# Eighteen experts' weights loaded as whole 4 MB matrices in 32 KB rows, instead of half matrices in a ring of nine pieces

## The reference

```python
h = rmsnorm(x, norm2_g)
# a router picks 2 of 32 experts for each token (4 groups of 8), with gates
h_e = silu(xb @ w_gate[e]) * (xb @ w_up[e])      # w_gate, w_up: 2048 x 512
y_e = h_e @ w_down[e]                            # w_down: 512 x 2048
x = x + sum over a token's experts of gate * y_e
out = rmsnorm(x, final_g)
```

## Time and profile before

| | |
|---|---|
| Median of 3 runs | 1319.04 us (1318.78 to 1321.24) |
| Profiled execution's own time | 1319.11 us |
| Its span, first to last instruction | 1317.4 us |
| TensorE busy | 1236.0 us (94%) |
| VectorE, ScalarE busy | 557.3 us (42%), 286.0 us (22%) |
| Moved by DMA | 471.76 MB, mean 358 GB/s over the span |
| Mean granted TensorE clock | 0.984 |

### The profile page before, as it was taken

The page is one execution under the profiler, slowest core; times in us unless marked ns, Lnnn a source line. Parts: engine busy times, 40 slices in busy tenths (PEclk is TensorE's granted clock), DMA queues, the critical chain, the costliest instruction groups (busy, mean ns, idle before and its releaser), DMA issues.

```text
span 1317.4 us, 15705 instructions
## 1 busy us (share of the span) xinstructions
PE 1236.0 (94%) x5942; PEld 647.5 (49%) x5942; DVE 557.3 (42%) x984; ACT 286.0 (22%) x401; POOL 6.0 (0%) x27
## 2 busy tenths in 40 slices
PE   8999999999999999999898899989988999998996
PEld 7888888888874333333333333333333333333332
DVE  6576988774565323232322223223222232232234
ACT  6443454474441011101001000010000000101003
POOL 1000000000000000000000000000000000000000
PEclk9999999999999999999999999999999999999998
DMA  8655454457489999999999999999999999999996
GB/s 306 218 190 178 144 192 162 158 180 300 159 337 344 432 430 430 430 431 432 432 430 430 433 431 432 431 430 432 430 433 431 430 431 432 432 432 430 428 428 251
DMA packets 65985, 471.76 MB, mean 358 GB/s; under 512 B 6135, under 2 KB 6647, under 8 KB 39452
## 3 DMA queue, kind: packets, MB, share of 16 engines
q1 hardware_dynamic: 65948, 471.24, 87.1%
HBM read 469.13 MB, written 2.10 MB: 358 GB/s over the span
## 4 chain that ended last, share of the span: by engine, by line
PE 61%; DMA 33%; DVE 2%; issue 2%; ACT 1%; DVEq 0%; SPq 0%; ACTq 0%
DMA ring<-in_w_up 22%; PE bank L1873 20%; DMA zone_u<-in_w_up 10%; PE bank L1627 10%; PE bank L1635 8%; PE bank L1909 7%; PE bank L1922 5%; PE bank L1636 4%; PE bank L1843 1%; PE bank L1874 1%; DVE zone_u L1056 1%; PE bank L1638 1%; DMA x_tok<-in_x 1%; PE bank L2066 1%; ACT gatesT L867 1%
## 5 line engine op out<-in xcount | busy, mean ns | idle before, releaser
L1873 PE MATMUL bank<-ring,win 128*64 128x512 f32 x816 | 377.3, 617 | 41.5 <-DMA ring<-in_w_up 29.0
L1874 PE MATMUL bank<-ring,win 128*64 128x512 f32 x832 | 378.6, 608 | 0.0
L1873 PEld LDWEIGHTS bank<-ring,win 128*64 128x64 f32 x816 | 111.9, 141 | 284.3 <-issue 265.6
L1635 PE MATMUL bank<-h_both,w_hi 128*128 128x512 f32 x540 | 192.7, 399 | 1.2 <-DVE h_both L978 1.0
L1428 DVE SCALAR_TENSOR_TENSOR x_tok<-bank,gate_of,x_tok 128x512 f32<-128x512 f32 x248 | 169.1, 744 | 30.2 <-PE bank L1922 29.2
L1909 PE MATMUL bank<-ring,hiddenT 128*64 128x512 f32 x672 | 150.8, 594 | 11.3 <-ACT gatesT L867 11.3
L409 DVE TENSOR_TENSOR w_lo<-stage,w_hi 128x2048 fp32r<-128x2048 f32 x58 | 132.5, 2291 | 64.1 <-ACT w_hi L403 64.0
L1636 PE MATMUL bank<-h_both,w_lo 128*128 128x256 f32 x540 | 151.4, 280 | 0.0
L403 ACT ACTIVATE w_hi<-stage 128x2048 fp32r<-128x2048 f32 x58 | 111.3, 1921 | 122.1 <-PE bank L1636 78.5
L859 ACT ACTIVATE rows_now<-bank,root_row 64x512 f32<-64x512 f32 x31 | 21.1, 681 | 533.5 <-PE bank L1874 533.5
L1922 PE MATMUL bank<-y_rows,gatesT 64*128 64x512 f32 x496 | 123.5, 615 | 0.0
(11 more groups left out here) (274 smaller groups left out, 1052.8 us busy)
## 6 DMA issues: line engine op xcount, KB each, us to landing
ring<-in_w_up SPq DMA_DIRECT2D x49, 2048.0 KB, 31.6
ring<-in_w_gate SPq DMA_DIRECT2D x47, 2048.0 KB, 34.9
ring<-in_w_down SPq DMA_DIRECT2D x41, 2048.0 KB, 31.6
stage<-in_w_in SPq DMA_DIRECT2D x43, 1024.0 KB, 5.1
zone_u<-in_w_down SPq DMA_DIRECT2D x19, 2048.0 KB, 31.7
zone_u<-in_w_up SPq DMA_DIRECT2D x9, 2048.0 KB, 33.6
zone_u<-in_w_gate SPq DMA_DIRECT2D x9, 2048.0 KB, 35.0
stage<-in_w_out SPq DMA_DIRECT2D x16, 1024.0 KB, 4.9
```

The lines of the kernel that those rows point to most:

```text
L1635: M.matmul(dst[:, :], hi[:, at], both, start=(c == 0), stop=False)
L1873: M.matmul(dst[0:W_ROWS, :], rows_of[:, c, 0:W_ROWS], gate[:, at], start=(c == 0), stop=(c == C - 1))
L1874: ins = M.matmul(dst[UPPER, :], rows_of[:, c, 0:W_ROWS], up[:, at], start=(c == 0), stop=(c == C - 1))
```

## The change

Experts 0 to 11 are loaded as before (`WIDE = 12`). For experts 12 to 29:

- Each matrix is one transfer of 4 MB, 128 partitions by 32 KB, into a pair of neighbouring buffers. `ring[0]` to `ring[6]` become parts of one tensor `ring_early`, so that pairs are contiguous. There are four pairs: gate of even experts in buffers 0 and 1, gate of odd experts in 7 and 8, up in 5 and 6, down in 2 and 3. Buffer 4 is unused.
- SP's order is gate, up, down of each expert. Gate waits for `down` of the expert two before; up waits for all four quarters of the expert before; down waits for `down` of the expert before.
- TensorE works in another order (`wide_expert`): it first scatters half 0 of the former expert, then waits for the gate matrix and the whole up matrix, does quarters 0 and 1, `turn_gates`, quarters 2 and 3, scatters half 1, `turn_hidden`, `down`.

Experts 30 and 31 get buffers of their own choice (`LAST_SLOTS`) and waits written out by hand; their transfers keep their sizes, their order, and TensorE's order of work, and expert 30's down pieces have semaphores of their own (`former_down`). The final norm's factors, the scratch of the final squares and the buffers of the crowded branch move to other slots.

```diff
-        ring = [sb(f"ring{k}", [P, PIECE]) for k in range(EARLY)]
+        ring_early = sb("ring_early", [P, EARLY * PIECE])
+        ring = [ring_early[:, k * PIECE:(k + 1) * PIECE] for k in range(EARLY)]
...
+LAST_SLOTS = ((0, 1, 4, 7, 8, 5), (6, 2, 3, 0, 1, 4))
+GATE_PAIRS, UP_PAIR, DOWN_PAIR = (0, 7), 5, 2
+WIDE = 12
+ROUNDS = WIDE // ROUND
+WIDE_ROUNDS = (E - 2 - WIDE) // 2
...
+        def pair(k):
+            whole, first = (ring_early, k) if k < EARLY else (zone_u, k - EARLY)
+            return whole[:, first * PIECE:(first + 2) * PIECE]
...
+            with sp.Fori(0, WIDE_ROUNDS) as i:
+                for r in range(2):
+                    e = i * 2 + (WIDE + r)
+                    gate, up, down = (a[n][0][bass.ds(e, 1)].rearrange("e (p x) n -> p (e x n)", p=P)
+                                      for n in ("w_gate", "w_up", "w_down"))
+                    sp.wait_ge(down_used, J * e - J)
+                    sp.dma_start(pair(GATE_PAIRS[r]), gate).then_inc(gate_loaded[r], 16)
+                    sp.wait_ge(in_used, QUARTERS * e)
+                    sp.dma_start(pair(UP_PAIR), up).then_inc(up_loaded, 16)
+                    sp.wait_ge(down_used, J * e)
+                    sp.dma_start(pair(DOWN_PAIR), down).then_inc(down_loaded, 16)
 
             def load_by_halves(e, src):
 
                 for first in (gate_first, gate_last):
-                    for k in (first, first + 1):
-                        wait_used(e + (k - RING) // PIECES, (k - RING) % PIECES)
+                    if e == E - 2:
+                        sp.wait_ge(in_used, QUARTERS * (E - 3 if first == gate_first else E - 2))
+                    else:
+                        sp.wait_ge(down_used, J * (E - 2))
+                        if first == gate_last:
+                            sp.wait_ge(in_used, QUARTERS * (E - 2) + 2)
...
             src = expert_pieces(E - 2)
             load_by_halves(E - 2, src)
-            for k in (down_first, down_last):
-                load_next(E - 2, k, slot_of(E - 2, k), src)
+            for h in range(2):
+                k = down_first + h
+                sp.dma_start(ring[slot_of(E - 2, k)], src[k]).then_inc(former_down[h], 16)
             src = expert_pieces(E - 1)
             load_by_halves(E - 1, src)
-            wait_used(E - 2, 2)
+            sp.wait_ge(in_used, QUARTERS * (E - 2) + QUARTERS)
...
+            def wide_expert(t, gate, of_gate):
+
+                up, weights = pair(UP_PAIR), pair(DOWN_PAIR)
+                banks_free(t - 1, 0)
+                scatter(t - 1, 0, BACK_BANK)
+                pe.wait_ge(win_ready, t)
+                of_gate()
+                pe.wait_ge(up_loaded, 16 * t - 16 * (WIDE - 1))
+                gate_up(t, 0, gate, up, win, whole=True)
+                gate_up(t, 1, gate, up, win, whole=True)
+                turn_gates(t)
+                gate_up(t, 2, gate, up, win, whole=True)
+                gate_up(t, 3, gate, up, win, whole=True)
+                banks_free(t - 1, 1)
+                scatter(t - 1, 1, BACK_BANK)
+                turn_hidden(t)
+
+                def arrived(j):
+                    if j == 0:
+                        pe.wait_ge(down_loaded, 16 * t - 16 * (WIDE - 1))
+
+                down(t, weights[:, 0:PIECE], weights[:, PIECE:], arrived)
+
+            with pe.Fori(0, WIDE_ROUNDS) as i:
+                for r in range(2):
+                    wide_expert(i * 2 + (WIDE + r), pair(GATE_PAIRS[r]), lambda: pe.wait_ge(gate_loaded[r], 16 * i + 16))
```

More of the change, by code:

```diff
@@ L53 @@
 HALVED = (8, 9, 10, 11, 12, 13, 14)
-CROWD_SLOTS = (0, 1, 5, 6, 7, 8)
-FINAL_SLOT = 2
+CROWD_SLOTS = (0, 1, 2, 4, 5, 7)
+FINAL_SLOT = 8
+LAST_SLOTS = ((0, 1, 4, 7, 8, 5), (6, 2, 3, 0, 1, 4))
+GATE_PAIRS, UP_PAIR, DOWN_PAIR = (0, 7), 5, 2
 ROUND = 3
@@ L64 @@
 RETURNS = 2 * BLOCKS
-ROUNDS = (E - 1) // ROUND
+WIDE = 12
+ROUNDS = WIDE // ROUND
+WIDE_ROUNDS = (E - 2 - WIDE) // 2
 assert MOE_BLOCK0 % 3 == 0 and PARTS == 3 and C % STAGES == 0
@@ L304, in hybrid_moe_program @@
         piece_loaded = [sem(f"piece_loaded{k}") for k in range(RING)]
+        gate_loaded = [sem(f"gate_loaded{r}") for r in range(2)]
+        up_loaded = sem("up_loaded")
+        down_loaded = sem("down_loaded")
+        former_down = [sem(f"former_down{h}") for h in range(2)]
         crowd_loaded = [sem(f"crowd_loaded{k}") for k in range(PIECES)]
@@ L377, in piece_at @@
             n = PIECES * e + k
-            assert n != LENT_PIECE
+            assert n != LENT_PIECE and e < WIDE
             if n < FIRST_LOADS:
@@ L385, in slot_of @@
         def slot_of(e, k):
-            return piece_at(e, k)[0]
+            return LAST_SLOTS[e - (E - 2)][k] if e >= E - 2 else piece_at(e, k)[0]
         def load(sp, b, chunks, first=0):
@@ L456, in load_piece @@
             def load_piece(k, src):
-                sp.dma_start(ring[k][:, :], src).then_inc(piece_loaded[k], 16)
+                sp.dma_start(ring[k], src).then_inc(piece_loaded[k], 16)
             gate_first, up_first, gate_last, up_last, down_first, down_last = range(PIECES)
@@ L538, in _ @@
                         load_next(e, k, slot_of(ROUND + r, k), src)
-            assert ROUNDS * ROUND == E - 2
+            assert ROUNDS * ROUND == WIDE and WIDE + 2 * WIDE_ROUNDS == E - 2
+            assert [n for n in (slot_of(WIDE - 1, k) for k in range(3))] == [DOWN_PAIR, UP_PAIR, UP_PAIR + 1]
+            with sp.Fori(0, WIDE_ROUNDS) as i:
[9 more added lines that the diff above has]
+                    sp.dma_start(pair(DOWN_PAIR), down).then_inc(down_loaded, 16)
             def load_by_halves(e, src):
                 for first in (gate_first, gate_last):
-                    for k in (first, first + 1):
-                        wait_used(e + (k - RING) // PIECES, (k - RING) % PIECES)
+                    if e == E - 2:
[4 more added lines that the diff above has]
+                            sp.wait_ge(in_used, QUARTERS * (E - 2) + 2)
                     for h in range(2):
@@ L573, in load_crowd @@
                 for k, src in enumerate(expert_pieces(e)):
-                    sp.dma_start(ring[CROWD_SLOTS[k]][:, :], src).then_inc(crowd_loaded[k], 16)
+                    sp.dma_start(ring[CROWD_SLOTS[k]], src).then_inc(crowd_loaded[k], 16)
             with sp.If(flag > 0):
@@ L900, in final_square @@
                 n = 2 * half + tile
-                nc.scalar.activation(ring[4][:, (BLOCKS * h + n) * NB:(BLOCKS * h + n + 1) * NB], x_tok[:, h, n * NB:(n + 1) * NB], ACT.Square,
+                nc.scalar.activation(ring[6][:, (BLOCKS * h + n) * NB:(BLOCKS * h + n + 1) * NB], x_tok[:, h, n * NB:(n + 1) * NB], ACT.Square,
                                      accum_out=sq_final[:, h, n:n + 1]).then_inc(done, 1)
@@ L1866, in sort, with gate_up @@
                         sort_part(c, t, z)
-            def gate_up(t, q, gate, up, rows_of, into=IN_BANK, part=range(C // QUARTERS)):
-                half, dst = (q % 2) * PART, bank[into]
+            def gate_up(t, q, gate, up, rows_of, into=IN_BANK, part=range(C // QUARTERS), whole=False):
+                half, dst = (q if whole else q % 2) * PART, bank[into]
                 for i in part:
@@ L2047, in _ @@
             turn_hidden(e)
-            down(e, piece(e, 4), piece(e, 5), arrived_down(e))
+            down(e, piece(e, 4), piece(e, 5), lambda j: pe.wait_ge(former_down[j // 2], 16))
             def last_turn(z):
```

## The result

The changed kernel takes 1329.49 us (median of 6 runs, 1324.44 to 1333.19), the one before 1319.22 beside it: ratio 1.0072, 95% interval 1.0061 to 1.0083. It is slower, as forecast, but by 10.3 us and not by 3.6, and outside the range. Its runs lie 9 us apart, those of before 2.5. The profiled execution took 1329.80 us, its span is 1328.1 us, 10.7 more than before.

The account below looks back on a forecast made before the run. DMA bytes were taken to bound the kernel up to expert 29's start, TensorE's work after it. Terms −2.1 + 9.7 − 1.9 − 1.8 − 0.3 = +3.6 us gave 1322.7 us, range 1320.0 to 1327.5.

Parts of the forecast that it names:

- What bounds the kernel, and where the end is decided: DMA bytes bound the experts' stretch; the end depends on expert 29's start and TensorE's work behind it.
- Term 1: Transfers before expert 29: 32 KB rows take 9.685 us per matrix for 9.725, over 53 transfers −2.1 us.
- Term 2: Quarter 0 of wide experts waits for the whole up matrix: +9.7 us, paid at expert 29.
- Term 3: Expert 29, start to scatter of half 1: scatter of half 0 leaves, −1.9 us; quarters at full clock, −1.8 us.
- the clock at expert 29: TensorE idles 0.9 and about 1.75 us, under 2.3, so no clock fall; the bound is one fall, +1.8 us.
- Term 4: Expert 31's last quarter: its stall for the last up piece goes, −0.3 us.
- Costed at nothing: does the queue stay full?: Wide experts' DMA queue stays full while 2.4 us remain; margin 2.2 us per expert, so no cost.
- Rival (d): The queue runs dry in each wide expert, from 2.2 us more in TensorE's path: 1348 or 1332 us; chance 0.08.
- Theory A: Formed after measuring: idle time at expert 12's start lets the clock fall, delaying later issues; 7.2 us of transfer time lost.

Follow-up runs that it names:

- f3_split_rows16: f2_split_up with gate and down also in two 2 MB transfers of 16 KB rows each; 1320.64 us.
- f2_split_up: The changed kernel with the up matrix in two 2 MB transfers, a semaphore each; quarters 0 and 1 need only the first; 1318.93 us.
- f1_keep9: The changed kernel with 9 idle-filling matmuls on TensorE between expert 11's down and the loop of wide experts; 1326.76 us.
- g2_late_up2: f2_split_up with SyncE issuing a wide expert's up matrix only after the second step of the former expert's down; 1338.33 us.
- e4_keep_old_order: e1_keep with 22 filling matmuls for 18 and scatter of half 0 back between turn_gates and quarter 2; 1371.17 us.
- e1_keep: The changed kernel with 18 matmuls, result unread, on TensorE between expert 11's down and the loop of wide experts; 1331.57 us.
- e3_keep_split_up: e1_keep with the up matrix in two 2 MB transfers, a semaphore each; quarters 0 and 1 need only the first; 1323.36 us.
- f4_split_old_order: f2_split_up with scatter of half 0 back between turn_gates and quarter 2; 1322.29 us.

## Why the prediction was wrong

- **What bounds the kernel, and where the end is decided**: right. Up to expert 29 bytes, then TensorE's own work. The end moved with expert 29's start in every kernel here.
- **Term 1, the rate**: right, 9.683 us for 9.685; f3 against f2 gave 0.041 us per matrix for 0.040.
- **Term 2, the whole up matrix**: right. Halving the wait moved expert 29's start from 1227.59 (f1_keep9) to 1223.09 (f2_split_up), 4.5 us. The forecast was 4.86 less 0.7 for the shorter rows, 4.2; the other 0.4 stood already at the handover, where expert 12's up matrix was whole at 733.56 in f1_keep9 and its first half there at 728.29 in f2_split_up, 5.27 and not 4.86 earlier.
- **Term 3 and the clock at expert 29**: right. The idle times there are 0.97 and 1.65 us, and the clock stayed up. **Term 4**: right that no wait for DMA is left in expert 31; from the scatter to its last quarter 0.14 us came back (50.07 for 50.21), not 0.3.
- **"Costed at nothing: does the queue stay full?"** is the step that failed: "the queue stays full while 2.4 remain". That figure came from one transfer into an empty queue, with nothing before it. It counts the time to the landing, and the landing is that of the slowest engine. In the running queue the 16 engines don't end together: of the transfer that landed at 873.2 the first engine ended its share 2.8 us before the landing and the last 0.3, by the packets in the trace; of the isolated one the first ended 0.75 us before it. A new transfer's first packet started 1.0 us after its issue in both. So in that place 2.8 + 1.0 = 3.8 us were needed for no engine to run dry, an estimate from this one trace. The 2.8 us are no constant: at other landings of the changed kernel they are 0.7 to 2.8 us, and in g2_late_up2, where it lost most, 2.8 to 3.6. Over 2.4 the forecast saw a margin of 2.2 us; over 3.8 it was under 1, and the slow clock after the handover took it: expert 13's up matrix was issued at 749.36, 1.2 us later than in f1_keep9, with 3.3 us ahead. g2_late_up2 and the steady state put what is needed over 3.2 and under 4.5. The Trainium skill, DMA: Bandwidth & Descriptors, section Anatomy of one DMA — SWDGE (gpsimd) path, gives a fixed cost of about 2.0 us for a transfer on the path that starts from GpSimd. The transfers here start from SyncE; the isolated one's 2.4 lie near that figure, but neither is the one for a queue that is to stay full.
- In the sum: 14.5 us later start of expert 29 (1234.33 for 1219.82) = 9.7 − 2.1 + 7.1, less 0.2: without the lateness the rate that was measured puts the landing at 1227.2, for the forecast's 1227.4. The term that was missing is the 7.1.
- **Rival (d)**, the queue runs dry, is what happened, in experts 13, 15, 17 and 19, and perhaps 14, and not in all 18. Its point of decision, "2.2 us more per expert", was too far off: 1.6 us less ahead than in the changed kernel's steady state (g2_late_up2, 3.2 for 4.8) and 1.9 us more in TensorE's path (e4_keep_old_order) were enough for losses in most experts, 1.1 and 2.4 us each on average.
- **Theory A** carries a part at most. With the clock kept up the ratio is 1.0054 [1.0039, 1.0068], without 1.0072 [1.0061, 1.0083] and 1.0063 [1.0039, 1.0086]; the intervals overlap. A slow clock matters only through the margin: with 9.7 us ahead (f2_split_up) it fell as well and cost nothing.

**Open.** Not every late landing fits the depth of the queue. In the changed kernel expert 14's up matrix was issued at 777.60, 5.9 us ahead of the landing before it (783.5), and landed 0.6 us late. In the first two experts after the handover one transfer lands 0.4 to 0.6 us late in most versions, however much lies ahead: 6.9 us in f2_split_up, 23 in f3_split_rows16. So a queue that runs dry is not what these show. The window of the changed kernel from 720 to 1220 us holds

```profile
q8 instruction: 2, 0.03, 0.0%
```

that is two 16 KB transfers of instructions, at 756.4 and 784.6 us. Every version with the wide loop has such a pair, one in each of its first two experts, and the kernel before has none from 640 to 1210. Each keeps one of the 16 engines 0.9 us. That they make a landing late is not shown; the 0.6 us of expert 14, and a part of what is lost at 13, may be theirs.

Nor does the depth say which landing is late: in the changed kernel an up matrix with 3.1 us ahead came on time (expert 15) and the down matrix after it, with 2.8, was 2.0 late. And why four of the unprofiled executions of f1_keep9 took 3.4 to 5.6 us more than its profiled one has no trace; that it is the queue is inferred from the spreads (f2_split_up 2.3 us, f1_keep9 5.8, e1_keep 16).

No version beat the kernel before. f2_split_up equals it: TensorE came to expert 31's last quarter just as its piece landed (it started at 1287.60 after scatter instructions begun at 1286.50 that need 0.96 us), so an earlier start of expert 29 or a faster transfer alone would gain 0.1 us. Both together would gain, as an estimate, the 0.7 us of term 1 that its 18 up matrices in 16 KB rows give away.

## What to carry to other kernels

When transfers are made larger and fewer, ask how many microseconds of bytes lie ahead at the moment of the latest issue, and compare that with a running queue and not with one transfer measured alone. Here splitting only the waits and the transfers of one of the three matrices raised it from 4.8 to 9.7 us, and the losses went. A longer wait for a larger piece costs nothing while bytes are the bound and all of it where the bound changes, here in the last three experts. Size the gain first: 5 ns per packet was all that 32 KB rows had to give, 2.1 us against 9.7.

## What was not expected of the hardware

- A running queue needs more bytes ahead than an isolated transfer's overhead says: 2.4 us for the isolated one, losses of 1.1 us per expert with 3.2 us ahead, none in the steady state with 4.5 to 4.9. The engines end a transfer up to 2.5 us apart in the changed kernel, 0.4 us in the isolated one.
- The fixed part of a packet is 5 ns from 8 KB to 32 KB rows: 306.4, 607.8 and 1210.4 ns (9.683 / 8) a packet.
- TensorE's clock (1.2 or 2.4 GHz): in the wide experts of all traces no idle time up to 1.78 us let it fall. From there to 3.5 us both came. It fell after 1.92 (e3_keep_split_up), 1.97 (changed kernel, to 913.25) and 3.33, and stayed after 2.00 (f1_keep9), 2.06 (changed kernel, to 972.93) and 3.51 (g2_late_up2, to 1030.54). After 7.74 us it stayed at 1.2 GHz until 736.3, 2.9 us into the work. In f4_split_old_order pieces of 2.6 to 2.7 us let it fall eight times of nine; in f2_split_up 0.97 and 1.68 with a scatter between them never did.
- Of two float32 matmuls, those that write different halves of a bank ran side by side (in e1_keep at 738.53 and 738.54, the next pair at 739.01 and 739.02); 36 instructions that write the same half took 0.43 us each.
